# Prompt attention of a fused decoder layer: two query tiles of one head in place of one query tile of two heads

## The reference, cut to what matters

```python
s = (jnp.einsum("bqhd,bkhd->bhqk", qn_b, k_nope)
     + jnp.einsum("bqhr,bkr->bhqk", qr_b, kr)).astype(jnp.float32) * MLA_SCALE
s = jnp.where(kpos[None, :] <= qpos[:, None], s, NEG)
p = jax.nn.softmax(s, axis=-1)
return jnp.einsum("bhqk,bkhd->bqhd", p.astype(v.dtype), v)
```

## Time and profile before

| | |
|---|---|
| median of 3 runs | 1804.6 us (1795.09 to 1806.44) |
| profiled execution, span from its first to its last instruction | 1796.1 us |
| TensorE busy, all of the span | 1722.8 us (96%) |
| VectorE busy | 858.5 us (48%) |
| ScalarE busy | 661.3 us (37%) |
| GpSimd busy | 578.2 us (32%) |
| mean granted TensorE clock | 0.98 |
| attention phase | about 254 to 868 us of the span |

### The profile page before, as it was taken

How to read it: one execution, slowest core, us unless ns; L and a number is a source line. 1 busy time by engine, 2 the same in 40 slices (tenths; PEclk the granted TensorE clock), 3 DMA queues, 4 the chain that set the end, 5 groups by cost and what they waited for, 6 DMA issues and landing times.

```text
span 1796.1 us, 27967 instructions
## 1 busy us (share of the span) xinstructions
PE 1722.8 (96%) x9949; PEld 1506.7 (84%) x9949; DVE 858.5 (48%) x1800; ACT 661.3 (37%) x1326; POOL 578.2 (32%) x535
## 2 busy tenths in 40 slices
PE   7999989999997999999999999999999999999996
PEld 6788878888886888888788989888898898888985
DVE  6433336667675776766443332433423333334235
ACT  5222125667675666565422312212112121121113
POOL 1000004566561877668301312212113122121221
PEclk9999987999999999999999999999999999999999
DMA  8232243323207565655612668486595775956812
GB/s 281 103 105 94 95 124 104 93 58 101 77 7 180 166 187 154 168 159 166 219 47 52 136 137 141 124 166 112 116 156 128 154 122 125 166 110 134 150 46 104
DMA packets 156061, 227.44 MB, mean 127 GB/s; under 512 B 31063, under 2 KB 128984, under 8 KB 149528
## 3 DMA queue, kind: packets, MB, share of 16 engines
q1 hardware_dynamic: 153086, 159.39, 30.0%
q0 software_dynamic: 2880, 66.85, 22.4%
HBM read 201.12 MB, written 91.93 MB: 163 GB/s over the span
## 4 chain that ended last, share of the span: by engine, by line
PE 48%; DMA 2%; ACT 1%; DVE 1%; POOL 0%; issue 0%; SPq 0%; ACTq 0%; DVEq 0%; POOLq 0%
PE wide L2582 22%; PE turn L2604 14%; PE rest L2583 7%; PE wide L2266 4%; DMA out_y_prompt<-f_gc 1%; PE wide L2681 1%; DMA o_work<-scratch_s_o 0%; DMA acc<-in_w_gate 0%; PE turn L2278 0%; DVE f_gc L2560 0%; ACT f_gc L2497 0%; PE rest L2589 0%; POOL f_gl L2660 0%; ACT f_rows L2504 0%; POOL f_st L2428 0%
## 5 line engine op out<-in xcount | busy, mean ns | idle before, releaser
L2604 PE MATMUL turn<-lead,f_ah 128*128 128x512 f32 x792 | 245.6, 391 | 4.7 <-DVE f_al L2548 4.0
L2517 DVE TENSOR_TENSOR acc<-turn,acc 128x512 f32<-128x512 f32 x198 | 136.6, 691 | 197.5 <-PE turn L2604 197.5
L2582 PE MATMUL wide<-hT_h,lead 128*128 128x512 f32 x704 | 184.9, 354 | 0.0
L2604 PEld LDWEIGHTS turn<-lead,f_ah 128*128 128x128 f32 x792 | 148.2, 189 | 36.5 <-DVE f_al L2548 4.2
L2385 POOL TENSOR_TENSOR f_gl<-f_graw,f_gh 128x1024 fp32r<-128x1024 f32 x21 | 50.6, 2408 | 351.6 <-ACT f_gh L2435 351.6
L1054 POOL TENSOR_SCALAR a_pr<-a_pr,a_rden 128x256 f32<-128x256 f32 (+7 forms) x128 | 94.3, 747 | 191.6 <-DVE a_rden L1154 187.0
L2604 PE MATMUL turn<-lead,f_al 128*128 128x512 f32 x396 | 154.8, 391 | 0.0
L2531 DVE SCALAR_TENSOR_TENSOR f_gc<-wide,f_coef,f_gc 128x832 f32<-128x832 f32 x44 | 47.7, 1085 | 209.6 <-ACT f_lasts L2455 206.7
L761 PE MATMUL zp<-win_h,xT_h 128*128 128x512 f32 (+1 forms) x288 | 113.0, 392 | 3.3 <-DVE acc L632 3.3
L761 PE MATMUL zp<-win_l,xT_h 128*128 128x512 f32 (+1 forms) x288 | 111.7, 388 | 0.0
L761 PE MATMUL zp<-win_h,xT_l 128*128 128x512 f32 (+1 forms) x288 | 111.7, 388 | 0.0
(11 more groups left out here) (362 smaller groups left out, 4437.3 us busy)
## 6 DMA issues: line engine op xcount, KB each, us to landing
out_s_win_k<-in_state_win_k POOLq DMA_DIRECT2D x10, 3264.0 KB, 41.8
out_s_win_v<-in_state_win_v POOLq DMA_DIRECT2D x10, 3264.0 KB, 44.4
acc<-in_state_win_k SPq DMA_DIRECT2D x16, 768.0 KB, 6.1
acc<-in_state_win_v SPq DMA_DIRECT2D x16, 768.0 KB, 5.6
f_uraw<-in_w_up SPq DMA_DIRECT2D x22, 512.0 KB, 4.4
f_draw<-in_w_down SPq DMA_DIRECT2D x11, 1024.0 KB, 33.0
f_graw<-in_w_gate SPq DMA_DIRECT2D x21, 512.0 KB, 7.9
acc<-in_cache_kv_latent SPq DMA_DIRECT2D x128, 64.0 KB, 1.8
```

The costliest lines, as they stand in the source:

```text
L2517: nc.vector.tensor_tensor(a, dp[h][:], a, ALU.add).then_inc(S["d_add"], 1)
L2582: nc.tensor.matmul(out[:, c0:c1], w[n][:, k, :], x[:, k, c0:c1], start=s, stop=e)
L2604: last = nc.tensor.matmul(dp[h][:], a[:, c, t * P:(t + 1) * P], w[:, c, h * 512:(h + 1) * 512], start=(c == 0 and j == 0), stop=(c == 1 an ...
```

## The change

A step becomes two tiles of 128 queries (2m and 2m+1) of one head. Steps 2m and 2m+1 of a pair are the same two tiles for the first and the second head. So there are again 8 steps for a pair and 64 in all, of 3, 3, 7, 7, 11, 11, 15 and 15 blocks of probabilities in place of 2, 4, 6, 8, 10, 12, 14 and 16. Scores, exponentials, multiplications and turns treat the same blocks as before. A turn's last unit has three blocks; there are as many units as before.

In the value product the weights are the values of one head with the high part in columns 0 to 63 and the low part in columns 64 to 127 (`a_vv`), and each key block takes two products, one with `a_ph` and one with `a_pl`, with 256 moving columns (two query tiles). The last key block is needed by the second query tile alone and takes two products with 128 moving columns. The upper and lower half of `a_o` are then to be added: ACT copies the lower half (64x256) to a new tile `a_low`, and DVE adds it to the upper half and writes `a_ot`. The product of low values with low probabilities, which was left out before, is now part of the sum.

```diff
-        self.vh = [sb(t(f"vh{i}"), [P, PT, 2 * HD], F32R) for i in range(2)]
-        self.vl = [sb(t(f"vl{i}"), [P, PT, 2 * HD], F32R) for i in range(2)]
+        self.vv = [sb(t(f"vv{i}"), [P, PT, 2, 2 * HD], F32R) for i in range(2)]
...
-        self.units = [(s + 2) // 2 for s in range(PT)]
+        self.units = [s // 2 + 1 for s in range(PT)]
...
+    def tile(self, s, j):
+
+        return s // 2 * 2 + j
+
+    def width(self, s, j):
+
+        return (self.tile(s, j) + 1) * P
...
+    def quarters(self, s, u):
+
+        return 4 if u + 1 < self.units[s] else 3
...
-            E.append((("value", k), 0.36 * (s + 1)))
+            E.append((("value", k), 0.24 * (self.tile(s, 0) + 1) + 0.22))
...
@@ scalar, "out"
-            if s % 4 == 0 and n:
-                act.wait_ge(S[f"o_out{s // 4}"], 16 * n)
-            nc.scalar.copy(self.ot[0:HD, s * P:(s + 1) * P], self.o_bank[0:HD, 0, :]).then_inc(S["o_a"], 1)
+            if k:
+                act.wait_ge(S["o_d"], k)
+            nc.scalar.copy(self.low[:], self.o_bank[HD:P]).then_inc(S["o_a"], 1)
...
@@ vector, "out"
-            dve.wait_ge(S["o_ps"], k + 1)
+            dve.wait_ge(S["o_a"], k + 1)
...
-            nc.vector.tensor_copy(self.ot[HD:P, s * P:(s + 1) * P], self.o_bank[HD:P, 1, :]).then_inc(S["o_d"], 1)
+            head, at = s % 2 * HD, self.tile(s, 0) * P
+            nc.vector.tensor_tensor(self.ot[head:head + HD, at:at + 2 * P].rearrange("p (j q) -> p j q", j=2),
+                                    self.o_bank[0:HD], self.low[:], ALU.add).then_inc(S["o_d"], 1)
...
@@ tensor, "value"
             if k:
-                pe.wait_ge(S["o_a"], k)
                 pe.wait_ge(S["o_d"], k)
...
-                for kb in range(2 * u, min(2 * u + 2, s + 1)):
-                    for i, (x, y) in enumerate(((vh, self.ph), (vh, self.pl), (vl, self.ph))):
-                        last = nc.tensor.matmul(self.o_bank[:], x[:, kb, :], y[:, kb], start=(kb == 0 and i == 0),
-                                                stop=(kb == s and i == 2))
+                if u + 1 < self.units[s]:
+                    terms = [(b, p) for b in (2 * u, 2 * u + 1) for p in (self.ph, self.pl)]
+                else:
+                    terms = [(both, self.ph), (both + 1, self.ph), (both + 1, self.pl), (both, self.pl)]
+                for b, p in terms:
+                    w = vv[:, b, s % 2, :]
+                    if b <= both:
+                        last = nc.tensor.matmul(out[:], w, p[:, b], start=(b == 0 and p is self.ph),
+                                                stop=(b == both and p is self.pl))
+                    else:
+                        last = nc.tensor.matmul(out[:, 1, :], w, p[:, b, 0, :], start=False, stop=False)
...
@@ LATENT_LATER
-    "scalar": {(0, "exp"): 1, (0, "out"): 6, ...
+    "scalar": {(0, "exp"): 1, (0, "out"): -1, ...
-    "vector": {(0, "out"): -3, ...
+    "vector": {(0, "out"): 2, ...
@@ DILATED_LATER
-        (1, "q_block"): 13},
-    "vector": {(1, "lead_rows"): -3, (0, "out"): -2, ...
+        (1, "q_block"): 8},
+    "vector": {(1, "lead_rows"): -3, (0, "out"): 2, ...
```

More of the change, by code:

```diff
@@ L895, in __init__ @@
         self.ident = io["ident_sb"]
+        self.low = sb(t("low"), [HD, 2, P])
         self.nm = sb(t("nm"), [P, 2, 2, 2])
@@ L940, in plan @@
         for k in range(2):
-            for h in range(2):
-                score(k, 0, h)
+            for j in range(2):
+                score(k, 0, j)
             E.append((("exp", k), 0))
@@ L969, in plan @@
             if k + 2 < self.STEPS:
-                todo = [(c, h) for c in range(len(self.chunks((k + 2) % PT))) for h in range(2)]
+                todo = [(c, j) for c in range(2) for j in range(2) if c < len(self.chunks((k + 2) % PT, j))]
             for u in range(self.units[s]):
-                E.append((("turn", k, u), 0.11 * 2 * min(2, s + 1 - 2 * u)))
+                E.append((("turn", k, u), 0.11 * self.quarters(s, u)))
                 if u >= 1 and todo and (u >= 3 or todo[0][0] == 0):
@@ L1003, in split, with turned @@
             self.ring.done(eng, e)
-    def turned(self, bank, m):
-        return bank[:, 0:m * 2 * P].rearrange("p (i h q) -> p i h q", i=m, h=2)
+    def turned(self, t, k, u):
+        return t[:].rearrange("p b j q -> p (b j q)")[:, 4 * u * P:(4 * u + self.quarters(k % PT, u)) * P]
     def bank_use(self, e):
@@ L1089, in scalar @@
             k = e[1]
[L1090 to L1096, removed]
+            for j in range(2):
+                last = len(self.chunks(k % PT, j)) - 1
+                self.ring.done(act, ("score", k, j, last))
+                p = self.pr[:, k % 2, j, 0:self.width(k % PT, j)]
+                nc.scalar.activation(p, p, ACT.Exp, bias=self.nm[:, k % 2, last, j:j + 1], scale=-1.0,
+                                     accum_out=self.den[:, k % 2, j:j + 1]).then_inc(S["exp"], 1)
         elif e[0] == "turn":
             _, k, u = e
-            m = min(2, k % PT + 1 - 2 * u)
             bank = self.ring.ready(act, e)
@@ L1128, in vector @@
             s = k % PT
-            c0, w = self.chunks(s)[c]
+            a = self.tile(s, h)
+            c0, w = self.chunks(s, h)[c]
             bank = self.ring.ready(dve, e)
@@ L1202, in tensor @@
             for i, (x, y) in enumerate(terms):
-                last = nc.tensor.matmul(out, x[r, h, rows], y[r, h, cols], start=(i == 0), stop=(i == len(terms) - 1))
+                last = nc.tensor.matmul(out, x[r, head, rows], y[r, head, cols], start=(i == 0), stop=(i == len(terms) - 1))
             last.then_inc(R["bank_ps"], 1)
@@ L1209, in tensor @@
             bank = self.ring.take(pe, e)
-            for i in range(min(2, k % PT + 1 - 2 * u)):
-                for h in range(2):
-                    last = nc.tensor.transpose(bank[:, (2 * i + h) * P:(2 * i + h + 1) * P],
-                                               self.pr[:, k % 2, h, (2 * u + i) * P:(2 * u + i + 1) * P], self.ident[:])
+            for q in range(self.quarters(k % PT, u)):
+                b, j = (2 * u + 1, 1) if q == 2 and self.quarters(k % PT, u) == 3 else (2 * u + q // 2, q % 2)
+                last = nc.tensor.transpose(bank[:, q * P:(q + 1) * P], self.pr[:, k % 2, j, b * P:(b + 1) * P], self.ident[:])
             last.then_inc(R["bank_ps"], 1)
@@ L1687 @@
     "sync": {(1, "setup"): -9},
-    "scalar": {(0, "exp"): 1, (0, "out"): 6, (1, "exp"): 5, (1, "o"): 5, (1, "p_new"): -2, (1, "pre_new"): 5,
+    "scalar": {(0, "exp"): 1, (0, "out"): -1, (1, "exp"): 5, (1, "o"): 5, (1, "p_new"): -2, (1, "pre_new"): 5,
         (1, "setup"): 8},
-    "vector": {(0, "out"): -3, (0, "over"): -2, (0, "prep"): 1, (0, "score"): -2, (0, "turn"): 1, (1, "cT"): 2,
+    "vector": {(0, "out"): 2, (0, "over"): -2, (0, "prep"): 1, (0, "score"): -2, (0, "turn"): 1, (1, "cT"): 2,
         (1, "p"): 3, (1, "pre_new"): 6, (1, "setup"): 9},
```

47 lines of the change are left out of this document (23 added, 24 removed).

## The result

The changed kernel takes 1820.9 us (median of 4 runs, 1815.7 to 1822.0), the kernel before 1803.4 us in the same comparison: a ratio of 1.0113, 95% interval 1.0092 to 1.0135. By the ratio it is slower by 20 us (of 1800), where 24 us less were forecast; the two medians themselves are 17.6 us apart, and the text goes by ratios throughout. The profiled execution's span is 1818.6 us.

The account below looks back on a forecast made before the run. TensorE, busy 96% of the span, was taken to bound the kernel. Savings of 24.5 and 1.0 us less 1.5 us of new waits gave 24.0 us less: 1804.6 to 1780.6, said as 1780 us; range 1761 to 1798.

Parts of the forecast that it names:

- part 3: Scores, turns, exponentials, normalising in the attention: same blocks, turn units and score banks in another order; counted as nothing.
- Part 1: Value products on TensorE: 0.120 us per 256-column product, 0.115 per 128-column one; 103.7 us become 76.2, 27.5 less.
- Part 2: Where value products lie: 89% in tight stretches, worth 24.5 us fully; a third of 3.0 us, 1.0, in loose ones.
- rival C: Thinner TensorE work makes the clock fall more often, losing 11 to 13 us of the gain: 1793 us; chance 0.06.
- Parts 4 and 5: Out on ACT and DVE: 0.5 us longer chain, covered by 3.5 us of TensorE work; 1.5 us new low-part waits.
- Part 6: Value split on POOL, once a pair: may take up to 3.4 us a pair more, hidden; ends nothing and 8 us.
- Rival B: TensorE waits before each value product for the previous step's addition; slower than before, 1830 us; chance 0.05.
- Rival A: Attention set partly by ACT and DVE chains; waits half eat the gain, 12 to 14 us gained, 1790 us; chance 0.19.
- The sign for a wrong prediction: TensorE's idle time in 289 to 520 and 580 to 840 us (17.5 us before) growing by more than 10 us.

Follow-up runs that it names:

- two-product kernel: The kernel before with the third value product of every key block (low values by high probabilities) left out: 1776.1 us, ratio 0.9871 to the kernel before.

## Why the prediction was wrong

The step that failed is part 3, "in another order. I count nothing". No reason stands behind that nothing. The change also rewrites the planned cost of the value product, which is a line of its diff, and the prediction has no term for it: it moves the work of the other side. The runs showed +17 us for it with copies side by side and +28 us with the new out. The account, each term from a pair of kernels that differ in it:

| term | forecast | measured |
|---|---|---|
| value products, off TensorE | -27.5 | -27.8 (two 128-column products take 0.225 us) |
| what a us of TensorE is worth | 0.89 and a third: -25.5 | 0.67: -18.7 |
| shape of the steps and new places of the out | 0 | +4.1 (what is left of 0.9919) |
| new out in series | +1.5 | +7.4 with the old cost (0.9960 over 0.9919), 18 with the new |
| planned cost | 0 | +27.6 (1.0113 over 0.9960) |
| sum | -24 | +20.4; the comparison has +20.3 |

The sum closes by construction, since each ratio is taken over the one before. The terms are good to some 3 us, the one with 0.67 to 5 by its interval, so the 4 us of the third row are not told from nothing. The last two rows are not independent: planned cost and new out cost 17 and 7 us each by itself and 35 together, so 11 us belong to their meeting.

- *Part 1* was right, pace of 256 columns and cost of 128 both. A single gap misleads here: in the changed kernel the first 128-column product starts its follower after 0.06 us, the second after 0.11, and the 256-column product behind them starts what follows after 0.18 and not 0.12 (679.57, 679.63, 679.74, 679.92 above). The two take 0.35 - 0.12 = 0.23 us, 0.115 each. Over all value products at full clock the whole product takes 0.12 us for each 256-column product and 0.30 us more, where it took 0.07 us more before; that is 0.11 us for each 128-column one. The short gap stood in the trace before as well, just ahead of the three that the prediction read:

```profile
651.43 0.22 PE L1203 MATMUL l_bank<-a_kh,a_qh 128*128 128x128 f32 x1
651.49 0.28 PE L1203 MATMUL l_bank<-a_kl,a_qh 128*128 128x128 f32 x1
```

  The Trainium skill gives 81 ns for such a product in a stream with loads of weights ("TensorE: Matmul & The Clock Gate", "Back-to-back issue gap"). This trace does not agree, and the measurement decides.
- *Part 2* was mis-sized: "there a microsecond of TensorE is a microsecond". 97% busy does not say so. With starts 0.12 us apart and products of 0.28 us, a gap of 0.15 us is still busy; that this is where the slack lay is argued. What the runs do show is that the clock took a part: the two-product kernel loses 42 us of full clock and the kernel before beside it 37, by the measure explained under rival C.
- *Parts 4 and 5* had the lengths of the instructions right and the cover wrong. 3.5 us between two value products is no cover if ACT is in two exponentials and the turns of the next step fill the ring. The series is 0.5 us longer a step, and 7 to 18 of the possible 32 us come through.
- *Part 6*: POOL's split kept its length (1051 and 2380 ns).
- *Rival B* came nearest in time, with 5% for it, and by luck: it had 26 us net from a chain wholly bare, and the chain cost 7 to 18 us. The sign that it named, tens of us of waits for the addition, did not show. *Rival A* knew that the order comes from planned costs, but not that the change rewrites one, and gained 12 us. The sign for a wrong prediction, idle time up by more than 10 us, did show: in the attention from 42 to 66 us.
- *Rival C* had a large part. By the prediction's own measure, length times what the granted clock lacks of 1, here over the whole span, an execution of the changed kernel loses 59 us of full clock (mean of its runs), one of the kernel before 34 to 37. In executions of the kernel before, which differ in nothing else that was changed, a microsecond of this measure went with 0.55 to 0.77 us of time. So by an estimate from these numbers 12 to 19 us of the changed kernel's time went by the clock, not far from C's price of 11 to 13. The kernel before with the new planned cost loses 56 us of full clock against 37, the changed kernel with the old cost 46. So the fall of the clock is not a cause beside the new order but in good part the way in which it costs. No run changed the clock alone, so the share stays an estimate.

## What to carry to other kernels

An order made from planned costs, with tables of places beside it, can belong to those costs: here one planned cost alone moved the time by 17 to 31 us. When an instruction gets cheaper, change the instruction and leave the plan, measure, and only then move the plan, alone. What TensorE is worth in a stage is to be measured by leaving some of its work out (here 0.67 us per us), not read from its busy share. What an instruction takes is to be read from a whole group, from its first start to the start behind it, not from one gap. And a result that was freed by two copies side by side should not be freed by two operations in series unless enough other TensorE work lies right behind the product (argued from the step above; even with the old order the series cost 7 us).

## What the runs showed of the hardware

Two 128-column products in a row with full loads of weights take 0.23 us together, counted to the start behind the group, where two of 256 columns take 0.24: half of the columns saved next to nothing. Gaps between starts alternate (0.06 and 0.11 us), and the product behind them pays (0.18). In the second stage the granted clock, the mean of its two levels, went with the idle time of the kernel: 0.98 with 27.5 us idle, 0.96 with 31.1, 0.92 with 38.4. In the first stage, which starts at half clock, it did not: 0.93 with 14.7, 0.93 with 27.3, 0.91 with 22.8. The same kernel, the one before, took 1789.0 us in an execution at a mean clock of 0.987 and 1803.1 us in one at 0.978.
